# A norm factor multiplied onto gate-up's tiles in the second block, and a one-column product inside gate-up and down

## The reference, cut to what matters

```python
def _rmsnorm(x, w):
    y = x * lax.rsqrt(jnp.mean(x * x, axis=-1, keepdims=True) + NORM_EPS)
    return y * w
def _causal_dwconv(x, w):            # K = 3: y[t] = x[t-2] w[0] + x[t-1] w[1] + x[t] w[2]
    ...
def _conv_glu_ffn(h, ffn_up, ffn_conv, ffn_conv_bias, ffn_down):
    u = _causal_dwconv(h @ ffn_up, ffn_conv) + ffn_conv_bias
    gate, val = jnp.split(u, 2, axis=-1)
    return (jax.nn.gelu(gate, approximate=True) * val) @ ffn_down
# second_block, one layer:
    h = _hybrid_mixer_2(_rmsnorm(x, pre_mix_norm[l]), ...)
    x = x + _rmsnorm(h, post_mix_norm[l])
    h = _conv_glu_ffn(_rmsnorm(x, pre_ffn_norm[l]), ffn_up[l], ...)
    x = x + _rmsnorm(h, post_ffn_norm[l])
# first_block, feed-forward part (twice a layer):
    x = x + 0.5 * (silu(gate) * up) @ w_down     # gate, up = split(_rms_norm(x, g) @ w_gu)
```

## Time and profile before

| | |
|---|---|
| time, median of three runs | 1983.71 us (1980.46 to 1986.99) |
| the profiled execution's own time | 1979.94 us |
| its span | 1978.1 us |
| mean granted clock of TensorE | 0.975 |
| TensorE busy | 1880.3 us, 95% |
| VectorE busy | 1214.3 us, 61% |
| ScalarE busy | 993.4 us, 50% |
| GpSimd busy | 722.0 us, 36% |

### The profile page before, as it was taken

How to read it: one execution, slowest core, us unless ns; L and a number is a source line. 1 busy time by engine, 2 the same in 40 slices (tenths; PEclk the granted TensorE clock), 3 DMA queues, 4 the chain that set the end, 5 groups by cost and what they waited for, 6 DMA issues and landing times.

```text
span 1978.1 us, 40944 instructions
## 1 busy us (share of the span) xinstructions
PE 1880.3 (95%) x15728; PEld 1842.6 (93%) x15728; DVE 1214.3 (61%) x1480; ACT 993.4 (50%) x1301; POOL 722.0 (36%) x607
## 2 busy tenths in 40 slices
PE   6999999999999999999999998997999889979997
PEld 6999999999999999999999997987999889969997
DVE  5655586666556545676665566556774755647754
ACT  4434565454454345555544456455654464556542
POOL 4760211257317621303376102513661105215631
PEclk9999999999999999999999989998999889999999
DMA  6646444455465556344464633222555323215543
GB/s 228 201 167 212 171 150 150 154 194 205 157 206 192 184 165 210 129 153 168 171 210 156 200 136 107 86 86 86 199 185 165 135 104 107 87 50 180 196 153 125
DMA packets 48938, 312.33 MB, mean 158 GB/s; under 512 B 5680, under 2 KB 6832, under 8 KB 19888
## 3 DMA queue, kind: packets, MB, share of 16 engines
q1 hardware_dynamic: 48096, 307.84, 45.6%
q10 hardware_dynamic: 720, 2.84, 0.4%
HBM read 309.61 MB, written 1.05 MB: 157 GB/s over the span
## 4 chain that ended last, share of the span: by engine, by line
PE 68%; DVE 10%; ACT 8%; DMA 6%; issue 5%; POOL 2%; ACTq 0%; DVEq 0%; SPq 0%; POOLq 0%
PE ps L558 18%; PE ps L559 18%; PE ps L560 18%; DMA raw<-in_down_dram 4%; ACT w_hi_w L1215 4%; DVE w_lo_w L1695 4%; PE ps L915 3%; PE ps L563 3%; PE ps L565 3%; PE ps L564 3%; DMA raw<-in_in_dram 1%; DVE v L2244 1%; DVE conv L2023 1%; PE ps L726 1%; PE ps L766 1%
## 5 line engine op out<-in xcount | busy, mean ns | idle before, releaser
L1695 DVE TENSOR_TENSOR w_lo_w<-raw,w_hi_w 128x2048 fp32r<-128x2048 f32 (+1 forms) x288 | 616.3, 2140 | 303.0 <-ACT w_hi_w L1215 302.3
L558 PE MATMUL ps<-xn,w_hi_w 128*128 128x256 f32 x2688 | 762.6, 284 | 39.9 <-DVE xn L1709 26.4
L559 PE MATMUL ps<-xn,w_hi_w 128*128 128x256 f32 x2688 | 753.8, 280 | 0.0
L560 PE MATMUL ps<-xn,w_lo_w 128*128 128x256 f32 x2688 | 753.6, 280 | 0.0
L1215 ACT ACTIVATE w_hi_w<-raw 128x2048 fp32r<-128x2048 f32 (+1 forms) x288 | 497.8, 1730 | 141.0 <-DMA raw<-in_down_dram 89.9
L558 PEld LDWEIGHTS ps<-xn,w_hi_w 128*128 128x128 f32 x2688 | 515.9, 192 | 47.8 <-DVE xn L1709 24.1
L559 PEld LDWEIGHTS ps<-xn,w_hi_w 128*128 128x128 f32 x2688 | 514.6, 191 | 0.6 <-issue 0.5
L560 PEld LDWEIGHTS ps<-xn,w_lo_w 128*128 128x128 f32 x2688 | 514.2, 191 | 0.0
L558 PE MATMUL ps<-h,w_hi_w 128*128 128x256 f32 x1056 | 294.2, 279 | 3.0 <-DVE w_lo_w L1695 3.0
L560 PE MATMUL ps<-h,w_lo_w 128*128 128x256 f32 x1056 | 293.8, 278 | 0.0
L559 PE MATMUL ps<-h,w_hi_w 128*128 128x256 f32 x1056 | 293.8, 278 | 0.0
(11 more groups left out here) (336 smaller groups left out, 2822.1 us busy)
## 6 DMA issues: line engine op xcount, KB each, us to landing
raw<-in_gu_dram SPq DMA_DIRECT2D x132, 1024.0 KB, 4.9
raw<-in_in_dram SPq DMA_DIRECT2D x68, 1024.0 KB, 4.9
raw<-in_down_dram SPq DMA_DIRECT2D x96, 704.0 KB, 4.1
raw<-in_out_dram SPq DMA_DIRECT2D x16, 1024.0 KB, 4.8
raw<-in_pb_dram SPq DMA_DIRECT2D x4, 1024.0 KB, 4.9
raw<-in_pa_dram SPq DMA_DIRECT2D x4, 1024.0 KB, 4.9
tables_all<-in_tables_dram ACTq DMA_DIRECT2D x1, 1648.0 KB, 6.8
rows<-in_rows_dram SPq DMA_DIRECT2D x2, 768.0 KB, 5.5
```

The source lines that it names most:

```text
L558: pe.matmul(out, w, xh, start=first, stop=False)
L559: pe.matmul(out, w, xl, start=False, stop=False)
L560: return pe.matmul(out, wl, xh, start=False, stop=last)
L1695: dve.tensor_tensor(in_ring(w_lo_ring, at, k)[:, 0:elems], raw[:, k % RAW_RING, 0:elems], in_ring(w_hi_ring, at, k)[:, 0:elems], ALU.subtr ...
```

## The change

It has two parts.

**A, the norm factor of the second block's gate-up.** xn becomes x x gain there too (`split_x` on ScalarE, `scale_low` on VectorE inside `post(1)`), rstd is not waited for ahead of the tiles, and VectorE multiplies it onto each of the two tiles of every slot, from PSUM into `conv_in`, before the taps; the taps read `conv_in` in SBUF. The mean square of x is no longer eight products of TensorE: GpSimd adds the eight squares (`post_square`, seven additions between and behind its residual additions), and one product (`mean_of_x`) stands in the middle of slot 1. The odd pieces' subtraction by GpSimd goes away. GpSimd's multiplication waits for the taps (`conv_ok`), no longer for `drained`.

**B, the one-column product.** `settle` is a float32 product of `ones_d` by one column of `ident` into a column of a bank that nothing reads at that point. It stands ahead of the fourth slot (j = 3) of every gate-up and ahead of the second tile of every down, in both blocks, after the waits that this slot or tile has anyway; so it runs 12 times. Slots 2 to 5 are therefore written out and the loop begins at slot 6.

```diff
-    v_ok = sig("v_ok", 0, KC)
+    post_sum = sig("post_sum", 0, KC - 1)
...
-    conv_ok = sig("conv_ok", 0, 36 + 3 * FC)
-    conv_src = sig("conv_src", 0, 6)
+    conv_ok = sig("conv_ok", 0, 36 + 4 * FC)
+    conv_src = sig("conv_src", 0, 6 + FC)
...
+        def settle():
+            pe.wait_ge(ready.sem, 16 * N_TABLES)
+            pe.matmul(ps[:, AUX + 1, 0:1], ones_d[:], ident[:, 0:1], start=True, stop=True)
+
+        def rest_of_gate_up(at, st):
+
+            for j in range(2, 6):
+                if j == 3:
+                    slot(at, st, j)
+                    pair(at, st, j)
+                    settle()
+                wide(at, st, j, 0, xn, KC)
+            with pe.Fori(0, (FC - 6) // 4) as g:
+                for j in range(6, 10):
+                    wide(at, st, j, g, xn, KC)
...
             wide(at, st, 1, 0, xn, KC, None, None, prev)
-            with pe.Fori(0, (FC - 2) // 4) as g:
-                for j in range(2, 6):
-                    wide(at, st, j, g, xn, KC)
+            rest_of_gate_up(at, st)
...
             tile(0, 0)
+            after(at, behind(prev), 1)
+            pe.wait_ge(lo.sem, lo.upto(at, st.slot0 + 3))
+            settle()
             tile(1, 0)
...
             mean_square(at, 0)
-            mean_square_direct(at, 1)
             first_wide(at, st2["gu"], 0)
...
+            def mean_of_x():
+                pe.wait_ge(post_sum.sem, post_sum.upto(at, KC - 1))
+                pe.matmul(ps[:, AUX, 0:T], ones_d[:], sq8[:, 0], start=True, stop=True).then_inc(mean_sq.sem, 1)
+
+            wide(at, st2["gu"], 1, 0, xn, KC, None, mean_of_x)
+            rest_of_gate_up(at, st2["gu"])
...
+            if f == 0:
+                before = 6 if st.name == "gu" else 0
+                act.wait_ge(conv_src.sem, conv_src.upto(at, before + j + 1 + 4 * g))
+            else:
+                act.wait_ge(drained.sem, drained.upto(at, st.free0 + j + 1 + 4 * g))
             if st.name == "gu":
-                tile_done(act, at, st, j, f, g)
-                src = ps[:, 2 * (j % 2) + f, 0:T]
...
                 x_ready(act, at, 0, c)
+                split_x(c, gains2[:, 4 * layer + 2, c:c + 1])
                 act.activation(sq8[:, c], x[:, c], ACT.Square).then_inc(squared.sem, 1)
+            open_rounds(at, st2["gu"], split)
             root(at, 2)
-            for c in range(KC):
-                act.wait_ge(v_ok.sem, v_ok.upto(at, c + 1))
-                copy(xn[:, c, 0], v[:, c]).then_inc(xn_hi.sem, 1)
...
-                whole = st.name == "gu"
-                if not whole:
-                    for f in range(2):
...
+                for f in range(2):
+                    tile_done(dve, at, st, j, f, g)
+                    dve.tensor_tensor(conv_in[:, j % 2, f], ps[:, 2 * (j % 2) + f, 0:T], rstd[:, 0:T], ALU.mult)\
+                       .then_inc((conv_src, drained)[f].sem, 1)
+                dve.wait_ge(drained.sem, drained.upto(at, st.free0 + j + 1 + 4 * g))
...
-                        src = ps[:, 2 * (j % 2) + f, 0:T - s] if whole else conv_in[:, j % 2, f, 0:T - s]
-                        ins = dve.scalar_tensor_tensor(c, src, w(f, last_tap - s), c, ALU.mult, ALU.add)
...
+                        dve.scalar_tensor_tensor(c, conv_in[:, j % 2, f, 0:T - s], w(f, last_tap - s), c,
+                                                 ALU.mult, ALU.add).then_inc(conv_ok.sem, 1)
...
                 def scale_next(c):
-                    if k == 3 and layer < DEPTH - 1:
-                        x_ready(dve, at, 1, c)
-                        scale_low(at, 1, c, gains2[:, 4 * (layer + 1), c:c + 1], xn_lo_odd if c % 2 else xn_lo_even)
+                    n = k // 2
+                    if k == 1 or layer < DEPTH - 1:
+                        x_ready(dve, at, n, c)
+                        scale_low(at, n, c, gains2[:, 4 * layer + k + 1, c:c + 1], xn_lo_odd if c % 2 else xn_lo_even)
...
-            for c in range(KC):
-                dve.scalar_tensor_tensor(v[:, c], x[:, c], gains2[:, 4 * layer + 2, c:c + 1], rstd[:, 0:T],
-                                         ALU.mult, ALU.mult).then_inc(v_ok.sem, 1)
...
-                    pool.wait_ge(drained.sem, drained.upto(at, st.free0 + i + 1))
+                    pool.wait_ge(conv_ok.sem, conv_ok.upto(at, 36 + 4 * j + 4 + 16 * g))
...
-            add_odd(at, 0)
-            for c in range(1, KC, 2):
-                low(at, 0, c)
+
+            def post_square(c):
+                pool.wait_ge(squared.sem, squared.upto(at, KC + c + 1))
+                if c > 1:
+                    pool.wait_ge(post_sum.sem, post_sum.upto(at, c - 1))
+                pool.tensor_tensor(sq8[:, 0], sq8[:, 0], sq8[:, c], ALU.add).then_inc(post_sum.sem, 1)
+
+            add_odd(at, 0, {3: (1,), 5: (2, 3), 7: (4, 5, 6, 7)}, post_square)
```

More of the change, by code:

```diff
@@ L1668, in gelu @@
             def gelu(j, g):
-                act.wait_ge(conv_ok.sem, conv_ok.upto(at, 36 + 3 * j + 3 + 12 * g))
+                act.wait_ge(conv_ok.sem, conv_ok.upto(at, 36 + 4 * j + 3 + 16 * g))
                 act.activation(silu_gate[:, j % 2], conv[:, j % 2, 0], ACT.Gelu_apprx_tanh).then_inc(gate_ok.sem, 1)
             act.activation(warm[:, 3:4], eps[:, 0:1], ACT.Gelu_apprx_tanh)
-            open_rounds(at, st2["gu"], split)
             rounds(act, at, st2["gu"], SLOT_DOWN, FC, split, gate_taps, gelu)
@@ L2003, in taps @@
             def taps(st, j, g, w, slots0, conv0, last_tap):
-                whole = st.name == "gu"
-                if not whole:
-                    for f in range(2):
-                        tile_done(dve, at, st, j, f, g)
-                        dve.tensor_tensor(conv_in[:, j % 2, f], ps[:, 2 * (j % 2) + f, 0:T], rstd[:, 0:T], ALU.mult)\
-                           .then_inc((conv_src, drained)[f].sem, 1)
-                    dve.wait_ge(drained.sem, drained.upto(at, st.free0 + j + 1))
-                per = 2 * last_tap - (1 if whole else 0)
+                for f in range(2):
[3 more added lines that the diff above has]
+                dve.wait_ge(drained.sem, drained.upto(at, st.free0 + j + 1 + 4 * g))
+                if st.name == "gu":
+                    dve.sem_inc(held.sem, 1)
+                per = 2 * last_tap
                 for s in range(1, last_tap + 1):
@@ L2021, in taps @@
                         c = conv[:, j % 2, f, s:T]
-                        src = ps[:, 2 * (j % 2) + f, 0:T - s] if whole else conv_in[:, j % 2, f, 0:T - s]
-                        ins = dve.scalar_tensor_tensor(c, src, w(f, last_tap - s), c, ALU.mult, ALU.add)
-                        if k < per:
-                            ins.then_inc(conv_ok.sem, 1)
-                        else:
-                            ins.then_inc(drained.sem, 1)
+                        dve.scalar_tensor_tensor(c, conv_in[:, j % 2, f, 0:T - s], w(f, last_tap - s), c,
+                                                 ALU.mult, ALU.add).then_inc(conv_ok.sem, 1)
             def decays():
@@ L2255, in _ @@
             split(at, so.slot0 + 3 + LEAD, 0, SLOT)
+            open_rounds(at, st2["gu"], split)
             inverse(at, 2)
-            for c in range(KC):
-                dve.scalar_tensor_tensor(v[:, c], x[:, c], gains2[:, 4 * layer + 2, c:c + 1], rstd[:, 0:T],
-                                         ALU.mult, ALU.mult).then_inc(v_ok.sem, 1)
-                if c >= 2 and c % 2 == 0:
-                    low_even(at, 0, c - 2)
-            low_even(at, 0, KC - 2)
             def gated2(j, g):
```

11 lines of the change are left out of this document (1 added, 10 removed).

## The result

The changed kernel takes 2000.41 us, median of five runs (1998.30 to 2002.91), against 1986.99 of the kernel before in the same comparison (1980.46 to 1990.25). The ratio is 1.0086, interval 1.0056 to 1.0115. I had forecast 1974 with a range of 1966 to 2003: the range holds the time, the sign is wrong. That the range holds it is luck, for its upper part stood there for rivals B and C, and it was neither. The profiled execution is the median one, 2000.41 us; against the profiled 1979.94 of before that is 20.5 more.

The account below looks back on a forecast made before the run. TensorE, busy 95% of the span, was taken to bound the kernel. 1979.9 - 8.7 (recovered pace) + 4.0 (one-column product) - 3.0 (second block, two layers) = 1972.2; with 1.9 for the runs' median 1974 us, range 1966 to 2003.

Parts of the forecast that it names:

- rivals B: Gate-ups and downs: the one-column product only draws TensorE's pace anew; carried over 1987 us; chance 0.20.
- D: TensorE's pace isn't set by interruptions, the one-column product only costs; carried over 1983 us; chance 0.07.
- it leaves the stream fast: Gate-up behind slot 3, down behind tile 1: every one-column product leaves TensorE's stream at 113.4 ns a product.
- rival C: The one-column product sets TensorE's slow pace each time, at all 12 places; 2011 us; chance 0.20.
- The gain: Slow products recovered behind the one-column product in gate-up and down: (1464 + 462) x 4.5 ns = 8.7 us.
- The cost: The one-column product adds 0.33 us at each of 12 places: +4.0 us, bounds 0 and 5.3.
- The entry: Start of the second block's gate-up: slot 1 5.1 us earlier, slot 2 3.8 us earlier, in each of two layers.
- the ring: Second block's gate-up: VectorE's multiplications, ScalarE's taps, w_hi, VectorE's split; 5.47 us against TensorE's 5.44, 0.5 us a layer.
- the three terms: Parts of the ring: multiplication to w_hi 1.26, w_hi 1.90, split to next VectorE operation 2.21 us.
- rival A: The ring becomes the bound, by taps meeting GpSimd's subtraction or slow pace after short waits; 1982 to 1992 us; chance 0.13.
- slack of 0.4: In the ring, four taps end at 2.7, w_hi at 3.16 us; so GpSimd's possible 0.5 us a round counted nothing.
- Down's first weights: End of second block's gate-up: w_hi of down's second slot comes later; +1.8 us a layer, bounds +0.5 and +4.

Follow-up runs that it names:

- e2: The kernel before with the one-column product alone (part B), slots 2 to 5 written out: 1980.70 us, ratio 0.9992.
- e5: The whole change with only ScalarE reordered, rounding weights one slot further ahead in the second block's gate-up: 2017.96 us, ratio 1.0180 to the kernel before.
- e8: e3 with ScalarE also rounding down's third piece of weights ahead of its last gelu: 1976.72 us, ratio 0.9962 to the kernel before.
- e10: e8 with the one-column product twice in gate-up (slots 3, 5) and moved from tile 1 to tile 2 in the second block's down: 1971.30 us.
- e3: The whole change with VectorE's weight split before its taps and ScalarE rounding one slot further ahead: 1978.23 us, ratio 0.9977 to the kernel before.
- e9: The whole change with only VectorE reordered, its split of the next weights between its multiplications and its taps: 2066.86 us (one run).
- e11: The kernel before with slots 2 to 5 of gate-up written out and no one-column product: 1988.47 us, ratio 1.0028.
- e12: e8 without the one-column product: 1980.61 us, ratio 0.9986 to the kernel before.

## Why the prediction was wrong

**The pace of TensorE: right in the main, and the rivals B, C and D fall.** I counted the starts of TensorE's products ahead of and behind each of the 114 one-column products in eight traces (the change, e2 to e5, e8 to e10). In a running stream, fast stayed fast 78 times of 78, and slow turned fast 16 times of 23. Where TensorE waited at the product, 5 of 7 fast streams came out slow and 2 of 4 slow ones fast; in two more, three products behind a wait, the pace ahead can't be read. Two places of the changed kernel, TensorE in time:

```profile
603.92 0.28 PE L560 MATMUL ps<-xn,w_lo_w 128*128 128x256 f32 x1
604.04 0.28 PE L599 MATMUL ps<-tables_all,ones_d 128*128 128x1 f32 x2
604.18 0.36 PE L558 MATMUL ps<-xn,w_hi_w 128*128 128x256 f32 x1
604.38 0.28 PE L559 MATMUL ps<-xn,w_hi_w 128*128 128x256 f32 x1
```

```profile
1807.96 0.28 PE L560 MATMUL ps<-xn,w_lo_w 128*128 128x256 f32 x1
1808.38 0.35 PE L599 MATMUL ps<-tables_all,ones_d 128*128 128x1 f32 x2
1808.59 0.36 PE L558 MATMUL ps<-xn,w_hi_w 128*128 128x256 f32 x1
1808.79 0.28 PE L559 MATMUL ps<-xn,w_hi_w 128*128 128x256 f32 x1
```

At the first the stream was slow and is fast from there on. At the second it was fast, waited 0.3 us, and is slow behind it. So "it leaves the stream fast" was nearly right, and what it misses is the wait, and the slow streams that stay slow: the changed kernel's first gate-up is one, with over 900 products at 118 ns. Against D stand the 13 of 13 slow streams that went on slow without the product. The 109 ns that the prediction took from the Trainium skill (TensorE: Matmul & The Clock Gate, "Back-to-back issue gap") stand there for a product by itself, with other figures for a stream; so they spoke neither for nor against two paces. The two few-column places of the earlier trace rows, which spoke for rival C, came behind queues of eight or more pieces; they didn't carry over to two pieces in a running stream. The gain was forecast as 8.7 less 4.0, that is 4.7; the runs give 4 to 5. The cost was mis-sized a little: 603.92 to 604.38 is 0.46, less two products of 0.118 is 0.22, against 0.33, 2.7 us for twelve. The mechanism behind the two paces stays open.

**The entry: right in kind, 1.0 and 1.3 us short.** Slot 1 came 4.1 earlier (forecast 5.1), slot 2 2.5 earlier (3.8, lower bound 2.5).

**The rounds: this step failed.** The prediction put it as "so the ring runs level with TensorE, 0.03 x 20 = 0.5 us a layer". Measured from slot 2 to slot 21 are 7.8 us a layer, for the ring takes 5.88 us and not 5.47. The ring was the right one, and the three terms were summed rightly; the first, 1.26, was read in the projections, where the code is written out and ScalarE's taps are 0.51 us long, and 0.05 was allowed for waits with registers. It is 1.73 in the loop and 1.53 in the gate-up's written-out rounds, so that even without the registers the ring would have been the bound (5.67). At 5.47 against 5.44 nearly any error upward falls wholly on the bound side: 0.4 us a round, times 20, times 2. I gave rival A (the ring becomes the bound) 0.13 and a price of 4 to 9 us a layer; the price of the rounds was right, its chance far too low, and its time of 1982 to 1992 too low, because down's first weights and the entry were mis-sized too. Of its two conditions the first came true, taps and GpSimd's subtraction meet in every round of the loop, but ScalarE's chain is as long without it; the slow pace of the second shows in 7 of 30 slots (6 to 20, both layers) and only shortens the wait behind them.

**GpSimd beside VectorE: weighed and then counted at nothing.** The Trainium skill (GPSIMD Engine Reference, "Key points") names contention between GpSimd and VectorE instructions with two SBUF inputs. The trace bears it out: the first tap at 1431.89 takes 1.02 us beside GpSimd's subtraction, and GpSimd's own multiplication 2.46 beside VectorE's split (0.73 in e9, where the split stands elsewhere). I had set the 0.5 us against a slack of 0.4 that VectorE's branch had behind ScalarE's; with ScalarE later by 0.47 and VectorE's first tap later with it, both branches end together, so it can't be charged apart.

**Down's first weights: +1.8 forecast, 4.7 measured** (bound +4; in the table +10.0 at tile 1 less the +5.3 at down's beginning). The late round brings the second slot's split late, as said, 4.3 us of wait instead of 1.2: 3.1 of the 4.7. The other 1.6 are a term that the sum didn't have, the granted clock of 0.50 behind that wait. The third slot's split is done at 1505.78, ahead of tile 1, which starts at 1508.68 without a wait.

Per layer that is -2.5 + 7.8 + 4.7 = 10.0 at tile 1, against a forecast of -1.5. For two layers the 11.5 make 23.0 of the 28.2 us between the sum of 1972.2 and the profiled 2000.41; by the end of down the recovered pace gives back a part.

## What to carry to other kernels

When a change adds an operation to a round, write down the ring that it closes (which engine waits for which, back to itself) and compare its length with the bounding engine's period. If they lie within a tenth, treat the ring as the bound (here 5.47 was computed and 5.88 came), and take each term from the same operations in a loop of the same form: register instructions alone were 0.20 us at one hand-over. Here order opened the ring, while a hand-over 0.20 shorter only brought it to 5.67; and both edges had to move at once, for each half alone was worse than neither. A wait that grows can cost more than its length, for TensorE's clock may come back low behind it. A product that shall restore TensorE's pace is better placed where the stream runs than behind a wait.

## What the hardware showed beyond that

TensorE's two spacings (113.4 and 117.9 ns for 128x256) persist over a thousand products; a two-piece product of one column in a running stream never made a fast stream slow (78 of 78) and made a slow one fast in 16 of 23, where without it 13 of 13 stayed slow. The same kernel's run-to-run spread, 28 us over 29 runs of the kernel before, is 12 over 12 runs of e10 (25 over 12 of e11 and 22 over 12 of e12, both without the product). Behind 4.3 us without work TensorE's granted clock read 0.50 and 16 products came 213 ns apart; behind waits of 1.2 to 1.9 us in the same place (before, e3, e8) it stayed at 1.00. A GpSimd operation that starts with a two-input VectorE operation in SBUF can lengthen either: tap 0.47 to 1.02, GpSimd's multiplication 0.73 to 2.46.
